# Layer norms of a two-block transformer kernel taken in two token halves

## What is computed

```python
h = layer_norm(h, ln_in_g, ln_in_b)
for l in range(2):
    h = layer_norm(ALPHA * h + 0.5 * swiglu_ffn(h, w13[l], w2[l]), ln_g[l, 0], ln_b[l, 0])
    mix = token_mix(h, w_in[l], ...)          # pooling, convolution, retention, then @ w_out
    h = layer_norm(ALPHA * h + mix, ln_g[l, 1], ln_b[l, 1])
    h = layer_norm(ALPHA * h + 0.5 * swiglu_ffn(h, w13b[l], w2b[l]), ln_g[l, 2], ln_b[l, 2])
return h[:, 16:]

def layer_norm(x, g, b):
    mu = mean(x); var = mean((x - mu) ** 2)
    return (x - mu) * rsqrt(var + 1e-5) * g + b
```

## Time and profile before

| | |
|---|---|
| median of 3 runs | 3303.19 us (3301.65 to 3304.37) |
| the profiled execution | 3299.9 us |
| its span, first to last instruction | 3297.9 us |
| PE busy | 3197.4 us (97%), 23670 matmuls |
| POOL busy | 1017.9 us (31%) |
| DVE busy | 993.0 us (30%) |
| ACT busy | 813.8 us (25%) |
| mean granted TensorE clock | 0.992 |

### The profile page before, as it was taken

One profiled execution on the slowest core, in us unless ns is written; L12 is line 12 of the kernel. 1 busy time (PEld: TensorE's weight loads), 2 busy tenths in 40 slices (PEclk: granted clock), 3 DMA queues, 4 the chain that ended last, 5 costly groups with the idle time before them and its releaser, 6 DMA issues.

```text
span 3297.9 us, 53285 instructions
## 1 busy us (share of the span) xinstructions
PE 3197.4 (97%) x23670; PEld 2569.7 (78%) x23670; DVE 993.0 (30%) x1676; ACT 813.8 (25%) x1058; POOL 1017.9 (31%) x449
## 2 busy tenths in 40 slices
PE   7999999989999989999999999999999999999998
PEld 4465688644444469999997999999999999778885
DVE  2144765541211241111463311113111154331113
ACT  2042412110000042222423422224222233242223
POOL 1020355200000024343463343434433346233431
PEclk9999999999999999999999999999999999999999
DMA  7541000249999942222221222222222222122221
GB/s 316 195 128 52 26 3 2 113 166 428 428 429 429 428 161 103 77 103 71 77 78 52 77 78 103 78 84 83 103 78 97 77 78 77 52 77 102 77 90 45
DMA packets 37745, 438.49 MB, mean 133 GB/s; under 512 B 5910, under 2 KB 6678, under 8 KB 11542
## 3 DMA queue, kind: packets, MB, share of 16 engines
q1 hardware_dynamic: 36088, 433.94, 33.4%
q10 hardware_dynamic: 1444, 1.36, 0.2%
HBM read 432.41 MB, written 2.10 MB: 132 GB/s over the span
## 4 chain that ended last, share of the span: by engine, by line
PE 60%; DVE 2%; ACT 1%; POOL 1%; DVEq 0%; issue 0%; ACTq 0%
PE PS L2343 42%; PE PS L2340 10%; PE PS L2582 2%; PE PS L2352 2%; PE PS L2154 1%; PE PS L2616 1%; PE PS L2600 1%; PE PS L2160 1%; DVE high L2214 1%; POOL w_lo L2330 1%; DVEq L2252 0%; ACT w_hi L2325 0%; PE PS L2577 0%; DVE low L2242 0%; PE PS L2625 0%
## 5 line engine op out<-in xcount | busy, mean ns | idle before, releaser
L2330 POOL TENSOR_TENSOR w_lo<-low,w_hi 128x2048 fp32r<-128x2048 f32 (+2 forms) x168 | 737.8, 4392 | 1663.5 <-ACT w_hi L2325 1663.1
L2343 PE MATMUL PS<-h_hi,w_hi 128*128 128x264 f32 x2736 | 560.6, 286 | 3.5 <-DVE h_lo L2923 3.4
L2343 PE MATMUL PS<-h_lo,w_hi 128*128 128x264 f32 x2736 | 558.4, 285 | 0.0
L2343 PE MATMUL PS<-h_hi,w_lo 128*128 128x264 f32 x2736 | 557.7, 285 | 0.0
L2343 PEld LDWEIGHTS PS<-h_hi,w_hi 128*128 128x128 f32 x2736 | 425.5, 188 | 9.0 <-issue 8.3
L2325 ACT ACTIVATE w_hi<-low 128x2048 fp32r<-128x2048 f32 (+2 forms) x168 | 306.8, 1826 | 493.6 <-PE PS L2343 397.4
L2343 PEld LDWEIGHTS PS<-h_lo,w_hi 128*128 128x128 f32 x2736 | 424.4, 188 | 0.0
L2343 PEld LDWEIGHTS PS<-h_hi,w_lo 128*128 128x128 f32 x2736 | 424.1, 189 | 0.0
L2452 DVE TENSOR_TENSOR low<-low,PS 128x528 f32<-128x528 f32 (+1 forms) x84 | 58.8, 700 | 778.1 <-PE PS L2343 575.8
L1795 PE MATMUL PS<-arena 128*64 128x512 f32 x1024 | 223.1, 593 | 0.4 <-DMA arena<-wts_dram 0.4
L2343 PE MATMUL PS<-g_hi,w_hi 128*128 128x264 f32 (+1 forms) x1056 | 221.8, 291 | 1.6 <-POOL w_lo L2330 1.6
(11 more groups left out here) (393 smaller groups left out, 4457.5 us busy)
## 6 DMA issues: line engine op xcount, KB each, us to landing
arena<-wts_dram SPq DMA_DIRECT2D x108, 2048.0 KB, 18.2
low<-wts_dram SPq DMA_DIRECT2D x70, 2048.0 KB, 7.8
arena<-wmod_dram SPq DMA_DIRECT2D x9, 2048.0 KB, 8.6
low<-wts_dram SPq DMA_DIRECT2D x12, 1536.0 KB, 6.4
arena<-na_bias_dram SPq DMA_DIRECT2D x16, 512.0 KB, 3.8
arena<-x_dram SPq DMA_DIRECT2D x2, 2048.0 KB, 8.3
low<-wts_dram SPq DMA_DIRECT2D x2, 1024.0 KB, 5.1
out_dram<-high SPq DMA_DIRECT2D x8, 256.0 KB, 2.4
```

The costliest lines, as they stand in the source:

```text
L2330: nc.gpsimd.tensor_tensor(lo, raw, hi.bitcast(F32), ALU.subtract).then_inc(w_l.sem, 1)
L2343: mm = nc.tensor.matmul(bank(b, h), w[wi], halves(x[xi])[:, h, :], start=(first and i == 0), stop=(last and i == 2))
```

## The change

1. **Groups.** `GROUPS` becomes 6, 8, 8 tiles: the group that a norm is woven into has 8 tiles in place of 6.
2. **The last units in halves.** In front of the five inner norms the units are `UNITS`: m = 0 to 5 whole, then (6, first half), (7, first half), (6, second half), (7, second half). A half unit has half of the matmuls. The mixer's last product uses banks 0 and 2 so that the statistics can lie in 4 and 5 in all norms.
3. **Statistics in halves.** `rest`, `square`, the moments, variance, root, reciprocal and the two spreads are done for the first half of the tokens during the units (6, second) and (7, second), and for the second half inside `first_two`. The places of PE's part are a table (`HOOKS`): `(m, half, tile) -> work`, behind that tile's matmuls.
4. **Scaling in halves.** `minus`, `scaled`, `h_hi` and the low parts are done for 264 tokens at a time, first half of all k, then second half. `first_two` follows in this order.
5. **Low parts.** POOL makes 12 of the 16 half low parts (all of the first half, four of the second), from 12 half copies of ACT; DVE makes the last 4.
6. **The second split.** ACT's `second_split` moves from behind the root to between the two halves, and POOL's from in front of its low parts to behind them, in the five inner norms.

The input norm keeps whole statistics and has only its scaling in halves. The last norm stays as it was.

The core of the diff:

```diff
-GROUPS = [(0, 8), (8, 8), (16, FT - 16)]
+GROUPS = [(0, 6), (6, 8), (14, FT - 14)]
...
+    UNITS = [(m, None) for m in range(6)] + [(6, 0), (7, 0), (6, 1), (7, 1)]
+    SQUARED = [(k, None) for k in (4, 0, 1, 2, 3, 5)] + UNITS[6:]
+    LOV, LOP = 4, 2 * DK - 4
+    R_BANK, S_BANK, E_BANK, I_BANK = 4, 5, (6, 7), (1, 4)
...
+    HOOKS = {(4, None, 6): [("spread",)],
+             (5, None, 4): [("rest", 4, None), ("square", 4, None)], (5, None, 6): [("square", 0, None)],
+             (6, 0, 1): [("square", 1, None), ("square", 2, None)], (6, 0, 4): [("square", 3, None)],
+             (6, 0, 6): [("rest", 5, None), ("square", 5, None)],
+             (7, 0, 2): [("rest", 6, 0)], (7, 0, 5): [("square", 6, 0)],
+             (6, 1, 1): [("rest", 7, 0)], (6, 1, 3): [("square", 7, 0)], (6, 1, 6): [("mean", 0)], (7, 1, 4): [("inverse", 0)]}
...
         ln_b.wait(dve, l, uu, 1)
         for k in range(DK):
-            scaled(k)
+            half_scaled(0, k)
+            if halved(l, uu) and k == 1:
+                evacuate(7, 1)
+            elif halved(l, uu) and k == 4:
+                variance(1)
+            elif halved(l, uu) and k == 5:
+                inverse(1)
             if k + 2 < DK:
-                minus(k + 2)
+                half_minus(0, k + 2)
+            else:
+                if k + 2 == DK:
+                    ln_eb.wait(dve, l, uu, 2)
+                half_minus(1, k + 2 - DK)
+            nc.vector.drain()
+        ln_b.wait(dve, l, uu, 2)
+        for k in range(DK):
+            half_scaled(1, k)
+            if k + 2 < DK:
+                half_minus(1, k + 2)
                 nc.vector.drain()
...
+        full_copy(0, DK - 1)
+        if halved(l, uu):
+            second_split()
+        for k in range(DK):
+            high_part(1, k)
             if 1 <= k <= DK - LOV:
-                nc.scalar.activation(hT[:, k - 1, :], res[:, k - 1, :], ACT.Identity, bias=shift[:, k - 1:k]).then_inc(ln_f.sem, 1)
+                full_copy(1, k - 1)
...
-        for k in range(DK - LOV):
-            ln_h.wait(pool, l, uu, k + 1)
-            ln_f.wait(pool, l, uu, k + 1)
-            nc.gpsimd.tensor_tensor(h_lo[:, k, :], hT[:, k, :], h_hi[:, k, :].bitcast(F32), ALU.subtract).then_inc(ln_lp.sem, 1)
+        for n, (h, k) in enumerate([(0, k) for k in range(DK)] + [(1, k) for k in range(DK - LOV)]):
+            ln_h.wait(pool, l, uu, h * DK + k + 1)
+            ln_f.wait(pool, l, uu, n + 1)
+            nc.gpsimd.tensor_tensor(part(h_lo[:, k, :], h), part(hT[:, k, :], h), part(h_hi[:, k, :], h).bitcast(F32),
+                                    ALU.subtract).then_inc(ln_lp.sem, 1)
+        second_split()
```

More of the change, by code:

```diff
@@ L2092, in sums, with part @@
         return PS[:, b, :] if fin else bank(b)
+    def part(ap, h):
+        return ap if h is None else ap[:, h * LH:(h + 1) * LH]
     class Sig:
@@ L2142, in centred, with lo_ready, quads @@
         else:
-            summed(eng, l, uu, k)
-    def lo_ready(eng, l, uu, k):
-        if k >= DK - LOV:
+            summed(eng, l, uu, k, h)
+    def lo_ready(eng, l, uu, h, k):
+        if h and k >= DK - LOV:
             ln_lv.wait(eng, l, uu, k - (DK - LOV) + 1)
         else:
-            ln_lp.wait(eng, l, uu, k + 1)
-    def quads(b, at, x, first, last, mean="mean_d"):
-        for j in range(4):
+            ln_lp.wait(eng, l, uu, h * DK + k + 1)
+    def quads(b, at, x, first, last, mean="mean_d", js=range(4)):
+        for j in js:
             mm = nc.tensor.matmul(PS[32 * j:32 * j + 32, b, at:at + QN], C[mean][:, 0:32], x[:, j * QN:(j + 1) * QN], start=first, stop=last)
@@ L2169, in stat_bank @@
     def stat_bank(l, uu):
-        return 2 if l is not None and uu == 1 else 4
+        return 4
     def ln_pe(pe, l, uu, at):
         sb = stat_bank(l, uu)
-        for kind, k in (LN_WORK_MIX if sb == 2 else LN_WORK).get(at, ()):
+        for kind, k in LN_WORK.get(at, ()):
             if kind == "first":
@@ L2192, in ln_pe @@
                     last.then_inc(ln_vp.sem, 1)
-        if at == "end":
+        if at == "end" and l is None:
+            ln_es.wait(pe, l, uu, 1)
+            for h in range(2):
+                spread_half(E_BANK[h], dq, h).then_inc(ln_eb.sem, 1)
+            ln_i.wait(pe, l, uu, 1)
+            for h in range(2):
+                spread_half(I_BANK[h], vq, h).then_inc(ln_b.sem, 1)
+        elif at == "end":
             ln_es.wait(pe, l, uu, 1)
@@ L2254, in ln_dve, with square, moments @@
         for k in range(DK - LOV, DK):
-            if not (l == NL - 1 and uu == 2):
-                low(k)
+            low(k)
     def ln_act(act, l, uu, next_split, second_split):
         shift = ln_shift(l, uu)
+        def square(n, k, h=None):
+            centred(act, l, uu, k, h)
+            nc.scalar.activation(part(sqT[:, k, :], h), part(res[:, k, :], h), ACT.Square).then_inc(ln_q.sem, 1)
+        def moments(h):
+            r = slice(64 * h, 64 * h + 64) if halved(l, uu) else slice(0, P)
+            nc.scalar.drain()
+            ln_ep.wait(act, l, uu, h + 1)
+            nc.scalar.activation(dq[r, :], PS[r, R_BANK, 256:256 + QN], ACT.Copy).then_inc(ln_es.sem, 1)
+            nc.scalar.activation(dsq[r, :], PS[r, R_BANK, 256:256 + QN], ACT.Square).then_inc(ln_es.sem, 1)
@@ L2271, in ln_act @@
[L2271 to L2278, removed]
+        nc.scalar.activation(cq, PS[:, R_BANK, 0:QN], ACT.Copy, scale=2.0).then_inc(ln_cs.sem, 1)
@@ L2279, in ln_act @@
+        if halved(l, uu):
+            for n, (k, h) in enumerate(SQUARED[0:6]):
+                square(n, k)
+            next_split()
+            square(6, 6, 0)
+            square(7, 7, 0)
+        else:
+            for n, k in enumerate(SQUARES):
+                if k == 5:
+                    next_split()
+                square(n, k)
+        moments(0)
+        root(0)
+        if last_norm(l, uu):
+            for k in range(DK):
+                ln_n.wait(act, l, uu, k + 1)
                 nc.scalar.activation(hT[:, k, :], res[:, k, :], ACT.Identity, bias=shift[:, k:k + 1]).then_inc(ln_f.sem, 1)
@@ L2334, in weights, with product @@
         return piece(i)[2:]
-    def product(b, w, x, first, last, fin=False):
+    def product(b, w, x, first, last, fin=False, hs=range(2)):
         for i, (wi, xi) in enumerate([(0, 0), (0, 1), (1, 0)]):
@@ L2390, in ffn_pe @@
                 i += 1
-            for m in range(DK):
-                if m % 2 == 0:
+            ending = g == len(GROUPS) - 1
+            for m, h in UNITS if ending and not fin else [(m, None) for m in range(DK)]:
+                if m % 2 == 0 and h != 1:
                     wt = [x.rearrange("p (m f n) -> p m f n", m=2, f=nf) for x in weights(pe, l, i)]
-                apart = 2 if g == len(GROUPS) - 1 else 4
+                apart = 2 if ending else 4
                 if m >= apart:
@@ L2809, in mix_pool @@
             mixed_lo(k)
-        for i in range(S_OUT + 2, S_FFN2 + 2):
+        for i in range(S_OUT + 2, S_FFN2 + 1):
             split_pool(pool, l, i)
```

278 lines of the change are left out of this document (196 added, 82 removed), and 4 rows, old and new, of the table FIRST_ORDER.

## The result

The changed kernel takes 3354.68 us (median of 4 runs, 3352.9 to 3359.08), the one before 3302.42 (4 runs): ratio 1.0163, 95% interval 1.0147 to 1.0179. So it is slower, as forecast, but by 52 us and not by 33, and outside the range. The profiled span grew from 3297.9 to 3352.9 us, by 55.0. The page, part 1, of the changed kernel, beside the earlier trace rows: PE does 48 matmuls more and is busy 37 us longer, so most of the loss is not idle time.

The account below looks back on a forecast made before the run. PE, busy for 97% of the span, was taken to bound the kernel. FFN norms +17.0, mixer norms +9.9, input norm +0.6 and clock +5.5, total +33, on 3303.2 gave 3336 us, range 3311 to 3345.

Parts of the forecast that it names:

- 2.1 reckoned: DVE's three waits in an inner norm: 0.2 last product, 0.6 second half's moments, 1.3 second half's inverse; 2.1 us.
- Rival (b): Inner norms: half operations cost half, DVE takes 0.73 us a step, PE runs straight through; 3290 us, chance 0.09.
- Rival (a): Inner norms: DVE and POOL don't get in each other's way, `w_lo` alone sets T + 20.0; 3324 us, chance 0.21.
- Rival (c): Inner norms: interruptions cost half, second piece in time, leaving DVE's T + 17; within 5 us of before, chance 0.10.
- Group sizes by themselves: the same matmuls, 0: FFN groups: the new sizes alone cost nothing, as matmuls stay the same and ACT's scaling is covered; 0 us.
- T to next piece, 22.0 and 1.1 for the clock: Each inner norm: 22.0 us from T to the next piece's first product, plus 1.1 us slow clock, +5.5 over five.
- the prediction's T: The end of the last product in front of a norm, from which the prediction counts its times.
- T later, 3.9 and 2.8: Ahead of inner norms: more interruptions of PE make T come 3.9 us later in FFN norms, 2.8 in mixer norms.
- 0.44: Ahead of inner norms: half a tile's statistics between products cost PE 0.32 for the interruption and 0.12 us more.
- for 0.6: Ahead of inner norms: a half spread costs PE 0.6 us, taken between 0.5 and a whole one's 1.1.
- Input norm +0.6: Input norm: 16 half steps in place of 8, but an earlier first part and cheaper low parts; +0.6 us.
- the 0.3 forecast for its `first_two`: Last FFN: `first_two` in halves takes 48 matmuls more of half the width; under 0.3 us.

Follow-up runs that it names:

- Experiment 1: The kernel before, with only the group sizes changed to 6, 8, 8: 3309.78 us against 3301.42, ratio 1.0024.
- experiment 4: The changed kernel with the same statistics in 9 places between products instead of 16: 3345.74 us, ratio 1.0128 to the kernel before.
- 5: The changed kernel with ACT's and POOL's second split earlier and PE's order of parts following it: 3338.55 us, ratio 1.0113 to the kernel before.
- 6: The changed kernel with the earlier second split of 5, the old groups 8, 8, 6 and statistics in 9 places (8 in the mixer): 3314.02 us.
- experiment 7: 6 with the second half's inverse spread earlier and two low parts moved from POOL to DVE: 3313.45 us, ratio 1.0035 to the kernel before.
- experiment 8: The kernel before, with its statistics merged from nine places between the products to four, in six norms: 3290.48 us against 3302.3, ratio 0.9966.
- experiment 9: experiment 8 with the tiles of every odd unit of a closing group reversed: 3283.79 us against 3299.54 for the kernel before, ratio 0.9952.
- experiment 2: The changed kernel with POOL's second split waiting until DVE's four low parts are done: 3355.43 us, ratio 1.0162 to the kernel before.
- 3: The changed kernel with PE's spread of the second half's inverse ahead of the first half's seventh high part: 3348.6 us, ratio 1.0139 to the kernel before.

## Why the prediction was right and wrong

**Direction.** Right, and for the reasons given. The gaps ahead of `first_two` go, the halves take 0.90 us a step, DVE's second half waits for the inverse (1.70 us; with the 0.69 for the moments its waits are 2.4 us, 2.1 reckoned), `w_lo` ends last and holds DVE's low parts. Rival (b), steps near 0.73 us, falls: 0.90. Rival (a), no collision, falls: 5.55 us for 1.71. Rival (c) falls with the time.

**Size: 22 us of the profiled 55 were not in the sum.** By its steps:

- *"Group sizes by themselves: the same matmuls, 0".* This is the step that failed worst. I counted matmuls and looked at ACT's cover for the scaling, not at the piece that PE needs behind the short tile, though that wait, 0.53 us, was there to be read in the trace of before. It is now 1.5 us longer in four FFNs, 6 us, and behind two of the four the clock is 0.58 and 0.56 for 3.6 us, some 3 us more. Experiment 1 measures +8.4 (5 to 11 by its interval). The windows behind the second and the third of the four waits, each of 2.03 us:

```profile
2215.80:2219.40 3.60, 3.56 (x18) 3.56 (x19) 0.70 (x1) 1.94 (x2) 1.59 (x1) 0.58 0.00 0
2626.20:2629.80 3.60, 3.52 (x29) 3.52 (x30) 0.70 (x1) 1.98 (x2) 1.57 (x2) 1.00 0.00 0
```

- *T to next piece, 22.0 and 1.1 for the clock.* From the prediction's T it is 23.53 on average, 0.43 more in each, 2.1 in all. Without the slow clock the chain takes 22.7 for 22.0, 3.5 us in all: POOL's ends at T + 20.8 and not at 19.9, DVE's last low part at T + 22.3 and not at 21.6. The clock costs 1.2 to 1.6 us behind each of the five gaps (12 to 16 matmuls 0.1 us further apart, in the last FFN where each is twice as long about half as many), 7.0 in all for 5.5. Of that only 4.1 falls ahead of the next piece; 1.0 falls on the second FFN, 0.4 on the second mixer, 1.4 on the last FFN, 0.1 on the first mixer.
- *T later, 3.9 and 2.8.* Without the group stall (1.5 each), one stretch of slow clock behind it (1.5), one gap of 1.34 and what the norms' own slow clock leaves there, it is 4.0, 3.9 and 3.6 in the FFNs, so right in size, and 3.6 in both mixers for 2.8. Half a tile's `quads` cost 0.54 and not 0.44, as much as a whole tile's: I had taken the tile's own share as proportional to its columns. Half spreads take 0.65 (1610.54 - 1609.89 is one) to 0.85, for 0.6. Both bear on FFNs and mixers alike; what makes up for them in the FFNs was not taken apart.
- *Input norm +0.6.* It is +1.6, and a wait of 1.34 us for `w_lo` in the piece behind it follows. No experiment tried it, but the trace shows both. The weight's low part still stands in front of the norm's here, and the new order asks for a low part after 12 matmuls where the old one had 32. So PE waits 1.22 us for POOL, and then runs on with hardly a gap (PE, then POOL):

```profile
1213.92 0.51 PE L2526 MATMUL PS<-h_lo,w_hi 128*128 128x264 f32 x2 [1.22 <-POOL h_lo L2465]
```

```profile
1208.59 4.57 POOL L2504 TENSOR_TENSOR w_lo<-low,w_hi 128x2048 fp32r<-128x2048 f32 x1 [7.26 <-ACT w_hi L2499]
1213.12 8.60 POOL L2465 TENSOR_TENSOR h_lo<-low,h_hi 128x264 fp32r<-128x264 f32 x12
1233.71 4.57 POOL L2504 TENSOR_TENSOR w_lo<-low,w_hi 128x2048 fp32r<-128x2048 f32 x1 [11.99 <-ACT w_hi L2499]
```

  The 1.34 us is ACT's: `scale_res`, 5.1 us, comes behind the norm's high parts and starts 2.2 us ahead of the next piece and not 3.7, so ACT copies the piece later, and POOL, idle for 11.99 us, ends its `w_lo` at 1238.28.
- *The first block*, whose code is the same, took 4.4 us more in this execution; in the executions of the other kernels it ended between 1186.9 and 1192.0 us. This is scatter, and no term of the change; by the medians the miss is 19 us and not 22. The last FFN and the end took 4.1 us more: 1.5 of stall, 1.5 of clock behind it and 1.4 of clock behind the norm's gap are more than that, so the 0.3 forecast for its `first_two` does not show.

What the experiments gave back fits: undoing groups, places and queue order (1, 4, 5, 6) brings 41 of 52 us. Of the 11 left after experiment 7, 2.7 are the input norm's, and 1.3 to 2.7 stand in each stretch ahead of a norm, where the half quads, the half spreads and the 64-row tile's two further appearances are; they were not taken apart. Halving a norm itself gives next to nothing back for these: 19.4 to 19.6 us against 20.1 to 20.7 in four of the norms is all that it gains in experiment 7.

## What to carry to other kernels

Before a size is changed "for free", look up which transfer or preparation ends just before its consumer at every seam that the size moves, and how much slack it has. Splitting work to start its consumer earlier pays only if the work behind it is not the true end: here the halves' cost on DVE (0.90 us a step, where half of a whole one would be 0.73) and a weight piece put behind twelve low parts took more than the wait that went. And count how often TensorE changes its tile shape, not how many small matmuls it does: gathering them in fewer places was worth 12 us with no other change, and pairing the 64-row tiles some 4 more, by the trace.

## What the runs showed of the hardware

- A change of TensorE from 128-row products to small tiles and back costs 0.32 to 0.39 us in the kernel before (experiment 8) and 0.30 to 0.32 in the changed one (experiment 4), besides the small matmuls themselves. A 64-row tile among 128-row ones costs 0.39 in the earlier trace rows; each one less saved 0.31 (experiment 9).
- DVE's operation with two SBUF operands and POOL's exclude each other for a whole instruction: 1.71 us of DVE's low parts became 5.55 (2), 6.50 (3). The Trainium skill (SBUF — State Buffer, "SBUF: two separate sides") calls it an exclusive lock of a shared port pair; the trace agrees. Removing the clash gained nothing here (3355.43 us against 3354.68), since it only decides which of the two comes first.
- The granted clock fell to its lower level for some 3 to 4 us (matmuls 0.22 us apart and not 0.12) behind each of the five waits of 3.5 us in the changed kernel and the five of 4.0 in experiment 2. Of the four waits of 2.03 to 2.33 us in the changed kernel two had it (0.58 and 0.56) and two had not (1.00). Which of these are hit was not settled; a stall's price here lies between its length and some 1.6 us more.
